# Rotary encoding's swap in a two-layer hybrid transformer kernel: from TensorE products to VectorE shuffles

## What is computed

```python
def _rope_axis(x, pos):
    half = x.shape[-1] // 2
    freqs = ROPE_BASE ** (-jnp.arange(half) / half)
    ang = pos[:, None] * freqs
    cos, sin = jnp.cos(ang)[:, None, :], jnp.sin(ang)[:, None, :]
    x1, x2 = x[..., :half], x[..., half:]
    return jnp.concatenate([x1 * cos - x2 * sin, x2 * cos + x1 * sin], axis=-1)

def axial_rope(x):
    t = jnp.arange(x.shape[1])
    half = x.shape[-1] // 2
    return jnp.concatenate([_rope_axis(x[..., :half], t // GRID_W), _rope_axis(x[..., half:], t % GRID_W)], axis=-1)
```

## Time and profile before

| | us |
|---|---|
| median of 3 runs | 1904.15 |
| lowest, highest | 1903.89, 1904.54 |
| profiled execution: span | 1903.9 |
| profiled execution: time of its own | not listed apart; its span lies between the lowest and the median run |
| PE busy in the span | 1764.5 (93%) |
| DVE busy | 739.2 (39%) |
| ACT busy | 400.7 (21%) |

### The profile page before, as it was taken

How to read it: one execution, slowest core, us unless ns; L and a number is a source line. 1 busy time by engine, 2 the same in 40 slices (tenths; PEclk the granted TensorE clock), 3 DMA queues, 4 the chain that set the end, 5 groups by cost and what they waited for, 6 DMA issues and landing times.

```text
span 1903.9 us, 30211 instructions
## 1 busy us (share of the span) xinstructions
PE 1764.5 (93%) x12970; PEld 815.2 (43%) x12970; DVE 739.2 (39%) x1647; ACT 400.7 (21%) x880; POOL 215.6 (11%) x300
## 2 busy tenths in 40 slices
PE   6999999999699999989998999989969999788888
PEld 3555657844333333323333555578532222222222
DVE  3982568812621212111114832588252222022222
ACT  3132246523100000000003213256330000000002
POOL 0000021110212121212011000021102000000000
PEclk9999999999799999999999899999989999999999
DMA  9743152022599999999998733130368999999996
GB/s 399 296 169 133 55 186 68 13 111 87 223 389 409 412 411 414 409 415 414 412 416 341 279 147 160 55 120 13 135 261 351 424 423 424 424 425 426 425 427 277
DMA packets 55143, 541.57 MB, mean 284 GB/s; under 512 B 7488, under 2 KB 9792, under 8 KB 24192
## 3 DMA queue, kind: packets, MB, share of 16 engines
q1 hardware_dynamic: 36720, 488.82, 62.0%
q0 software_dynamic: 18176, 51.26, 8.1%
q10 hardware_dynamic: 144, 0.01, 0.0%
HBM read 516.34 MB, written 23.72 MB: 284 GB/s over the span
## 4 chain that ended last, share of the span: by engine, by line
PE 71%; DMA 19%; DVE 7%; ACT 2%; issue 1%; POOL 0%; SPq 0%; DVEq 0%; POOLq 0%; ACTq 0%
PE ps L2272 19%; DMA ring<-in_wstream 10%; PE ps L1890 9%; PE ps L2340 8%; PE ps L2116 7%; PE ps L1865 6%; DMA big<-in_wstream 4%; PE ps L2060 3%; PE ps L2226 2%; DMA cst<-in_wstream 2%; PE ps L2347 2%; PE ps L2033 1%; PE ps L2026 1%; PE ps L1999 1%; DVE work L1196 1%; DVE big L1196 1%
## 5 line engine op out<-in xcount | busy, mean ns | idle before, releaser
L2272 PE MATMUL ps<-ring,work 128*32 128x512 f32 x4000 | 439.5, 594 | 24.1 <-DMA ring<-in_wstream 21.4
L1670 DVE TENSOR_TENSOR work<-glao,ps 128x512 f32<-128x512 f32 x32 | 22.0, 688 | 682.0 <-ACT glao L988 682.0
L2272 PEld LDWEIGHTS ps<-ring,work 128*32 128x32 f32 x4000 | 128.3, 110 | 331.1 <-issue 292.0
L1890 PE MATMUL ps<-hT,ring 128*128 128x512 f32 (+1 forms) x496 | 176.7, 514 | 2.1 <-issue 2.1
L2340 PE MATMUL ps<-big,work 128*32 128x512 f32 x1408 | 158.9, 593 | 6.6 <-DVE work L1672 6.6
L2116 PE MATMUL ps<-ring,hT 128*128 128x512 f32 x320 | 138.8, 592 | 0.0
L1890 PEld LDWEIGHTS ps<-hT,ring 128*128 128x128 f32 x496 | 94.3, 191 | 83.0 <-issue 74.8
L988 ACT ACTIVATE glao<-ps 128x512 f32<-128x512 f32 x32 | 19.1, 597 | 507.3 <-PE ps L2272 507.3
L1865 PE MATMUL ps<-ring,hT 128*128 128x384 f32 (+3 forms) x384 | 111.3, 451 | 0.0
L656 POOL DMA_INDIRECT big<-xn_lat,rows_q x64 | 62.6, 979 | 348.7 <-DVE work L1654 300.3
L2116 PEld LDWEIGHTS ps<-ring,hT 128*128 128x128 f32 x320 | 60.3, 191 | 72.2 <-issue 72.2
(11 more groups left out here) (336 smaller groups left out, 2167.4 us busy)
## 6 DMA issues: line engine op xcount, KB each, us to landing
ring<-in_wstream SPq DMA_DIRECT2D x146, 2048.0 KB, 19.9
big<-in_wstream SPq DMA_DIRECT2D x62, 2048.0 KB, 24.8
cst<-in_wstream SPq DMA_DIRECT2D x10, 2048.0 KB, 38.0
work<-in_wstream SPq DMA_DIRECT2D x10, 1024.0 KB, 36.1
hT<-in_wstream SPq DMA_DIRECT2D x10, 1024.0 KB, 32.8
x_kept<-big POOLq DMA_DIRECT2D x14, 512.0 KB, 3.0
big<-x_kept POOLq DMA_DIRECT2D x12, 512.0 KB, 5.9
work<-in_nat_bias POOLq DMA_DIRECT2D x32, 128.0 KB, 2.4
```

Source lines behind the costliest of these rows:

```text
L1890: last = T.matmul(bank(n % 4, tn), uw[:, j * D + kc * P:j * D + kc * P + P], hTv[:, kc, t0:t0 + tn], start=kc == 0, stop=kc == KC - 1)
L2272: last = T.matmul(bank(t)[32 * g:32 * g + 32, :], XST[:, e, t, kc, :], gate_up[j][kk][:, g * 512:(g + 1) * 512], start=kc == 0, stop=kc == ...
```

## The change

The swap product, its matrix in the constants and its waits on PE are removed. DVE does the swap with a shuffle inside each 32 partitions (partition m takes m xor 16); the sign that the matrix carried is now in the sine table, negative for the first 16 of each 32 partitions. The five rotations run ahead of the state steps instead of one after each, and each waits for its own block's copy (`proj_out`). The first part of `gla_state`, which makes the decayed keys and clears the states, is now `gla_state_begin` and stays ahead of the rotations. The second and third pass of a rotation no longer use the `link` chain but a semaphore of their own. The constants have 128 columns less.

```diff
-C_ID, C_HM, C_SUM, C_MF, C_MB, C_COS, C_SIN, C_ROT = 0, 128, 132, 148, 276, 404, 916, 1428
-CONST_FIRST, CONSTS = C_MF, C_ROT + P
+C_ID, C_HM, C_SUM, C_MF, C_MB, C_COS, C_SIN = 0, 128, 132, 148, 276, 404, 916
+CONST_FIRST, CONSTS = C_MF, C_SIN + LAT
+SWAPPED = [m ^ 16 for m in range(32)]
...
-            def gla_state(l):
+            def gla_state_begin(l):
...
                 V.memset(STATE[0][:, F_ORD[0], :], 0.0)
                 link(V.memset(STATE[1][:, B_ORD[0], :], 0.0))
+
+            def gla_state(l):
+
                 dve.wait_ge(sem("tot_exp"), 1 + l * PER["tot_exp"])
...
                     if i < 2:
                         query_args(l, i)
-                    rope(l, i)
 
             def rope(l, i):
 
                 b = [SK, SQ, SQ + 1, SQ + 2, SQ + 3][i]
-                dve.wait_ge(sem("rot"), i + 1 + l * PER["rot"])
-                V.tensor_tensor(ROT, bank(6 + i % 2), cst[:, C_SIN:C_SIN + LAT], ALU.mult)
-                link(V.tensor_tensor(FM[:, b, 0:LAT], FM[:, b, 0:LAT], cst[:, C_COS:C_COS + LAT], ALU.mult))
+                items = n_items(l, 1) if b == SK else n_items(l, 3) + (i - 1) * len(token_parts(l, False)) + 1
+                done = 3 * i + l * PER["rope_step"]
+                dve.wait_ge(sem("proj_out"), items + l * PER["proj_out"])
+                V.stream_shuffle(ROT, FM[:, b, 0:LAT], SWAPPED).then_inc(sem("rope_step"), 1)
+                dve.wait_ge(sem("rope_step"), done + 1)
+                V.tensor_tensor(ROT, ROT, cst[:, C_SIN:C_SIN + LAT], ALU.mult).then_inc(sem("rope_step"), 1)
+                V.tensor_tensor(FM[:, b, 0:LAT], FM[:, b, 0:LAT], cst[:, C_COS:C_COS + LAT], ALU.mult).then_inc(sem("rope_step"), 1)
+                dve.wait_ge(sem("rope_step"), done + 3)
                 V.tensor_tensor(FM[:, b, 0:LAT], FM[:, b, 0:LAT], ROT, ALU.add).then_inc(sem("rope"), 1)
...
+                gla_state_begin(l)
+                for i in range(5):
+                    rope(l, i)
                 gla_state(l)
...
                         if unit == 4 and i < STEPS:
                             state(l, i)
-                            rot(l, i)
...
-            def rot(l, i):
-
-                b = [SK, SQ, SQ + 1, SQ + 2, SQ + 3][i]
-                if i == 0:
-                    pe.wait_ge(sem("proj_out"), n_items(l, 4) + l * PER["proj_out"])
-                if i == 1:
-                    pe.wait_ge(sem("modrow_out"), DVE_GROUP[l] + 2)
-                if i >= 2:
-                    pe.wait_ge(sem("rope"), i - 1 + l * PER["rope"])
-                T.matmul(bank(6 + i % 2), cst[:, C_ROT:C_ROT + P], FM[:, b, 0:LAT], start=True, stop=True).then_inc(sem("rot"), 1)
...
-    c[:, C_SIN:C_SIN + LAT] = np.sin(ang)
-    for m in range(P):
-        if m % (2 * quarter) < quarter:
-            c[m + quarter, C_ROT + m] = -1.0
-        else:
-            c[m - quarter, C_ROT + m] = 1.0
+    c[:, C_SIN:C_SIN + LAT] = np.sin(ang) * np.where(np.arange(P) % (2 * quarter) < quarter, -1.0, 1.0)[:, None]
```

More of the change, by code:

```diff
@@ L115 @@
 PER = {"z": 2, "z_out": 2, "softplus": 2, "scan": 12, "totc": 2, "ke_arg": 2, "ke_exp": 2, "ke": 2,
-       "tot_exp": 1, "keT": 3, "keT_out": 1, "dSm": 10, "dS": 5, "state": 10, "rope": 5, "rot": 5,
+       "tot_exp": 1, "keT": 3, "keT_out": 1, "dSm": 10, "dS": 5, "state": 10, "rope": 5, "rope_step": 15,
        "q_arg": 6, "q_exp": 6, "qk": 6, "gla_ms": 1, "gla_rms": 1, "gate_silu": 1, "gate_gain": 1 + NT,
```

## The result

| | before | after |
|---|---|---|
| median, us | 1904.02 (4 runs) | 1891.29 (4 runs) |
| lowest to highest | 1903.73 to 1904.54 | 1889.46 to 1895.94 |
| ratio, 95% interval | | 0.9944 (0.9929 to 0.996) |
| profiled execution: time, span | not listed, 1903.9 | 1889.92, 1888.0 |
| PE busy in the span | 1764.5 | 1746.8 |

Two executions of the study, of 2657 and 10360 us, were disturbed and are left out of everything that follows.

A forecast was written before the change was run, and what follows sets the result against it. PE was taken to bound the projections, with swap products on its path. 1903.9 - 8.6 = 1895.3 us of span, with other terms at nothing, and 0.25 us to the median gave 1895.5; range 1893.5 to 1898.0.

The forecast's parts named there:

- What bounds the kernel: Layer projections: PE is busy every microsecond and swap products lie on the path; in expert stages the weight stream sets pace.
- What is removed: Projection stretches: ten swap products at 0.86 us start to start, so PE gives back 8.6 us, 4.3 in each layer.
- What is added and moved: DVE rotations: a shuffle of about 0.7 us makes each 2.7 us, hidden in DVE's waits; cost on the path nothing.
- What is late next: First intra-chunk scores: PE waits for ACT's last copy; layer 1's query scalings keep a 2.0 us margin, so no gain lost.
- Downstream: Expert weight stream: loads wait on attention and output projection, so 4.3 us pass in each layer; smaller constants taken as 0.
- How the numbers follow: Whole kernel: forecast has 91 in 100; its width comes from start-to-start reading, constants, runs and clock, one-sided towards less gain.
- the clock: Between attention and experts: clock averages 0.83, and shifting idle stretches could be worth perhaps 1 us in a layer.
- the runs 0.65 us between lowest and highest: Whole kernel before the change: spread of its three runs, taken as a 0.65 us part of the forecast's width.
- 1: Projection stretch: swap products are already hidden in PE's gaps, so the time stays 1904.15 us; 3 in 100.
- 2: Expert stages: one layer's gain is lost in the weight stream, giving 1899.8 us; 4 in 100.
- 3: DVE before the state steps: shuffles above 7.6 us queue up and slow the kernel, 1913 us at 12; 2 in 100.
- What would show it: Trace signs: first scores at 241.4 and 1228.7, PE busy down about 8.6 us, expert stretches 4.3 and 8.6 us earlier.

The follow-up runs named there:

- e_filler: Changed kernel with a same-shape product, its result unread, in each place where a swap product stood, both layers: median 1903.23 us, ratio 1.000.
- f_l0: Changed kernel with unread products of the same shape in the swap products' places in layer 0 only: median 1895.76 us, ratio 0.9979.
- f_l1: Changed kernel with unread products of the same shape in the swap products' places in layer 1 only: median 1896.22 us, ratio 0.9968.
- the filled ones: Kernels before and changed, each with unread products added in seven more of PE's waits: medians 1896.81 and 1896.71 us before, 1888.06 and 1888.54 us changed.
- e_inplace: Changed kernel, shuffles kept and no swap products, but each rotation left behind its state step: median 1889.51 us, ratio 0.9931.

## Why the prediction was right or wrong

**What bounds the kernel: right.** PE's order in the projection stretch set the end. The fillers put 10.5 +- 2.3 us back, all that the change had taken (10.5 +- 1.6).

**What is removed: right to 0.02 us.** 0.86 us a product from start to start; 8.58 in the two stretches, in every profile of the changed kernel. The busy time of a row (592 ns twice) would have given 11.8.

**What is added and moved: right.** 0.73 us a shuffle (0.7 taken, between 0.68 and 1.1). The lower bound was misread: 0.68 us isn't the cheapest pass of 128x512 in the trace of before, its copy at L1283 takes 0.43. Nothing hung on it. The last rotation ends 9.1 us ahead of the first step in layer 0 and 5.6 in layer 1. The Trainium skill ("VectorE: DVE Perf Modes", section "The perf-mode tier table") led to an estimate of 0.6; the measured 0.73 is a fifth more and nearer to the transpose of the earlier trace rows. The cost on the path is nothing. What I didn't see is that one pass of each layer would take 3.40 and 2.84 us instead of 0.7 (last section); the cover took that too.

**What is late next: right.** PE waits for ACT's copy, 0.47 and 0.69 us, as before. In layer 1 the scalings end at 1220.51, 2.04 us ahead of PE's start; the prediction had a margin of 2.0. With the rotations left in place it would have been the scalings, 1.03 us later.

**Downstream: right.** Neither expert stage gave anything back (lengths within 0.2 us), the queue's waits for the output projection are 234.3 us in both profiles and for attention 102.8 and 103.3, and each layer's filler costs about its 4.3.

**How the numbers follow: wrong, in two terms.** The first is the clock: "worth perhaps 1 us in a layer (my estimate; a change of 0.01 in that mean over 80 us)", and "one-sided towards less gain". The row that I took it from, 460 to 540 us, is one of several places where PE waits and its clock falls. Measured, one such place alone, between the layers, is worth 4.4 us, and with all of them the same kernel varies by 8 to 10 us from execution to execution. The term was too small by a factor of four or more and it has both signs, and I had no reason to make it a loss only. Nor was the range worked out from it: it went 2.0 us below the forecast and 2.5 above, where the terms named add up to 2.9.

The second is "the runs 0.65 us between lowest and highest". Three executions of before were close together at 1904.15, near the upper one of two groups (mean of 72: 1902.7, from 1897.84 to 1906.45). I took them as the kernel's width. I also read the profiled span as lying 0.25 us under the median, when the time of an execution is its span plus 1.9 to 2.0: it was one of the slowest. With the pooled mean as base, the sum gives 1902.7 - 8.6 = 1894.1. The changed kernel's mean of 1892.2 is 1.9 us under that, and under the range too. So of the 4.2 us that the median of four lay under the forecast, 1.45 are the base that happened to be high, 1.9 are the unfilled kernels' difference beyond 8.6, and 0.9 are this median's place under the mean. None of it is in the stretches that the change touches.

**The rivals.** 1 fell by `e_filler`, 2 by `f_l0` and `f_l1` and the lengths of the stages, 3 by the shuffle's 0.73 us (it needed 7.6) and the idle time of DVE ahead of the first state steps.

**What would show it.** The pairs, the shuffles, the waits and the DMA share of the expert stretches came as named. Three things didn't, and I put them down to the clock. The first scores of layer 1 start at 1222.55, not 1228.7 (those of layer 0 at 240.77, not 241.4). The expert stages begin 6.0 and 15.7 us earlier, not 4.3 and 8.6. PE's busy time fell by 17.7 us, not 8.6: the same 64 transposes take 10.29 us at the lower clock and 7.38 at the upper, so busy time contains the clock as well.

**Open.** The unfilled kernels differ by 10.5 +- 1.6, the filled ones by 7.9 +- 0.95. The intervals overlap, so the 2.6 us between may be nothing. I put them down to the clock, since at equal mean clock (0.980, by the fit) the unfilled kernels are some 9 us apart, but why the changed kernel falls into the faster group more often (13 of 18 against 30 of 72) isn't settled, and with 18 executions part of it may be chance. That the start time of the waits sets where the clock falls was argued, not shown: no run moved them without changing the work. The profiles of the same or nearly the same load with either distance between the layers agree with it, and say no more.

## What to carry to other kernels

Price a removed matmul by the distance from start to start around it, and check that the wait which ends last behind it moves along; that gave the size of this change to a fiftieth of a microsecond in the stretch where it acts. Before a forecast of a few tenths of a per cent, look at how far a dozen or more executions of a kernel lie apart, and list every stretch in which PE waits and its clock is at the lower level: what such stretches change from execution to execution (here 8 to 10 us) is the width of the forecast, in both directions, however sure the mechanism. Products that keep PE occupied in those waits are worth trying for themselves: here they gave 6.3 us before and 3.6 after the change, the filled changed kernel is the fastest seen (1888.06 and 1888.54 us, ratios 0.9925 and 0.9927), and with them a small change can be measured with about half the spread or less (standard deviations of 2.3 and 3.3 us against 1.3 and 1.2).

## What the runs showed that was not expected

One pass of DVE in each layer takes several times as long as its like. The timeline of DVE at the first rotation of layer 0, in the profile of the changed kernel:

```profile
156.12 0.73 DVE L1273 STREAM_SHUFFLE glao<-big 128x512 f32<-128x512 f32 x1
156.88 0.69 DVE L1275 TENSOR_TENSOR glao<-glao,cst 128x512 f32<-128x512 f32 x1
157.49 3.40 DVE L1276 TENSOR_TENSOR big<-big,cst 128x512 f32<-128x512 f32 x1
160.92 0.69 DVE L1278 TENSOR_TENSOR big<-big,glao 128x512 f32<-128x512 f32 x1
...
1160.75 2.84 DVE L1276 TENSOR_TENSOR big<-big,cst 128x512 f32<-128x512 f32 x1
```

The last row is the same pass in layer 1. POOL beside them, in both layers:

```profile
157.31 3.02 POOL L595 TENSOR_TENSOR big<-big,prm 128x1536 f32<-128x1536 f32 x1 [84.76 <-ACT big L818]
...
1160.20 2.84 POOL L595 TENSOR_TENSOR big<-big,prm 128x1024 f32<-128x1024 f32 x1 [113.40 <-ACT big L818]
```

The multiplication with the cosine takes 3.40 and 2.84 us, where the eight others of that line take about 0.68. POOL's instruction runs from 157.31 to 160.33 and from 1160.20 to 1163.04; 0.68 after its end is 161.01 and 1163.72, and DVE's ends at 160.89 and 1163.59. So DVE did its pass after POOL's instead of beside it. The pass is as long in layer 0 in all eight profiles of kernels that rotate ahead of the state steps (3.39 to 3.40 us). It goes the other way too: POOL's two instructions take 3.02 and 2.84 us here and 2.90 and 2.34 in `e_inplace`, where no rotation stands beside them. Here they begin 0.26 and 0.63 us before the end of DVE's multiplication with the sine, and are 0.12 and 0.50 us longer. The Trainium skill ("SBUF — State Buffer", section "Who interferes with whom") says that a DVE instruction with two SBUF inputs contends with a GpSimd instruction that reads SBUF, and calls the port pair that they share an exclusive lock. The trace agrees in which instructions are longer and in which order; each of the four numbers is 0.12 to 0.14 us less than a wait for the end of the other's row would give. In `e_inplace` all ten passes with the cosine take 0.68 to 0.69 us. No run took POOL's instruction away, so the cause is read from the times and the page, not shown by itself. It cost nothing, because DVE idles there; on a path of DVE it would be 2.7 and 2.2 us for one instruction.
